# A hybrid decoder layer: the attention norm's scales are spread by DMA instead of by TensorE transposes

## What is computed

```python
h = rmsnorm(x, norm_g)
proj = h @ w_in                       # 1024 -> 8704, split in 12 pieces
y_a = (silu(layernorm(conv31(a_val * sigmoid(a_gate)))) * silu(a_z)) @ w_a_out
o = diff_attention(q, k, v, lam)      # 4 heads, causal: (softmax(q1 k1) - lam softmax(q2 k2)) v
o = rmsnorm(o, subln_g, 1e-5) * (1.0 - lam_init)   # over the 128 channels of a head
y_b = (o * silu(b_z)) @ w_b_out
y_c = (c_b * conv3(c_c * c_x) * silu(c_z)) @ w_c_out
merged = g0 * y_a + g1 * y_b + g2 * y_c            # sigmoid gates
out = rmsnorm(x + merged @ w_o, final_g)
```

## Time and profile before

| | us |
|---|---|
| median of 3 runs (2297.95 to 2299.34) | 2298.78 |
| the profiled execution | 2299.36 |
| its span, first to last instruction | 2297.6 |
| TensorE matmul busy, of the span | 2265.2 (99%) |
| VectorE busy | 1424.9 (62%) |
| ScalarE busy | 755.8 (33%) |
| GpSimd busy | 230.1 (10%) |
| mean granted TensorE clock | 0.999 |

### The profile page before, as it was taken

The page is one execution under the profiler, slowest core; times in us unless marked ns, Lnnn a source line. Parts: engine busy times, 40 slices in busy tenths (PEclk is TensorE's granted clock), DMA queues, the critical chain, the costliest instruction groups (busy, mean ns, idle before and its releaser), DMA issues.

```text
span 2297.6 us, 29108 instructions
## 1 busy us (share of the span) xinstructions
PE 2265.2 (99%) x10864; PEld 1836.2 (80%) x10864; DVE 1424.9 (62%) x2706; ACT 755.8 (33%) x1610; POOL 230.1 (10%) x186
## 2 busy tenths in 40 slices
PE   7999999999999999999999999999999999999998
PEld 6888888878888888888787787888877787778886
DVE  4767667774665665564566657665456656577752
ACT  4333332342333331022344344102135455441021
POOL 3545300100000000010000000001000000000010
PEclk9999999999999999999999999999999999999999
DMA  8877788788554545566644454456664444435555
GB/s 310 291 263 266 269 290 290 281 324 313 187 179 175 181 168 183 188 253 248 254 175 172 168 183 147 165 200 239 247 256 157 166 157 156 154 129 179 188 192 201
DMA packets 90604, 490.77 MB, mean 214 GB/s; under 512 B 9312, under 2 KB 9568, under 8 KB 45408
## 3 DMA queue, kind: packets, MB, share of 16 engines
q1 hardware_dynamic: 90464, 488.90, 59.6%
HBM read 375.61 MB, written 113.25 MB: 213 GB/s over the span
## 4 chain that ended last, share of the span: by engine, by line
PE 94%; DVE 3%; DMA 1%; issue 1%; ACT 0%; SPq 0%; DVEq 0%; ACTq 0%
PE PJ L733 73%; PE SC L792 6%; PE SC L824 5%; PE TB L833 3%; PE OB L857 1%; PE OB L858 1%; PE OB L792 1%; PE PJ L792 1%; PE OB L860 1%; PE OB L859 1%; DMA Wp<-split_weights 1%; PE TB L868 0%; DMA PX<-x_t 0%; DMA UC<-x 0%; PE TB L876 0%
## 5 line engine op out<-in xcount | busy, mean ns | idle before, releaser
L733 PE MATMUL PJ<-hT,Wp 128*128 128x512 f32 x6480 | 1577.4, 395 | 1.1 <-DMA Wp<-split_weights 0.6
L733 PEld LDWEIGHTS PJ<-hT,Wp 128*128 128x128 f32 x6480 | 1187.7, 188 | 254.0 <-issue 17.7
L1493 DVE SCALAR_TENSOR_TENSOR ACCS<-UA,col,ACCS 128x512 f32<-128x512 f32 x464 | 348.8, 793 | 0.4
L1030 ACT ACTIVATE PX<-SC,negm 128x512 f32<-128x512 f32 (+3 forms) x320 | 195.9, 623 | 153.3 <-DVE negm L1329 153.1
L1374 DVE TENSOR_TENSOR ZA<-TB,ZA 128x512 fp32r<-128x512 f32 (+1 forms) x144 | 95.0, 660 | 172.7 <-ACT ZA L1050 171.8
L1329 DVE TENSOR_REDUCE negm<-SC 128x2 f32<-128x1024 f32 (+3 forms) x160 | 168.9, 1061 | 43.0 <-PE SC L824 40.7
L1050 ACT ACTIVATE ZA<-TB 128x512 fp32r<-128x512 f32 (+1 forms) x144 | 82.5, 573 | 308.1 <-PE TB L833 308.1
L1089 ACT ACTIVATE TG<-PJ,col 128x512 f32<-128x512 f32 x64 | 44.1, 688 | 341.2 <-PE PJ L733 341.2
L1367 DVE SCALAR_TENSOR_TENSOR PX<-PX,sc 128x512 f32<-128x512 f32 (+3 forms) x160 | 105.4, 680 | 52.7 <-ACT PX L1041 52.1
L792 PE MATMUL SC<-Wp,KM 128*128 128x512 f32 x384 | 121.4, 389 | 0.0
L1041 ACT ACTIVATE PX<-PX,sc 128x512 f32<-128x512 f32 (+3 forms) x160 | 98.6, 655 | 64.6 <-DVE sc L1356 44.3
(11 more groups left out here) (191 smaller groups left out, 2044.6 us busy)
## 6 DMA issues: line engine op xcount, KB each, us to landing
Wp<-split_weights SPq DMA_DIRECT2D x264, 1024.0 KB, 4.8
split_weights<-Wp SPq DMA_DIRECT2D x88, 1024.0 KB, 4.9
Wraw<-w_stream SPq DMA_DIRECT2D x88, 512.0 KB, 5.9
KM<-keys SPq DMA_DIRECT2D x24, 512.0 KB, 5.7
VM<-values SPq DMA_DIRECT2D x24, 512.0 KB, 6.0
PX<-x SPq DMA_DIRECT2D x16, 512.0 KB, 7.0
out<-PX SPq DMA_DIRECT2D x16, 512.0 KB, 10.8
keys<-KM SPq DMA_DIRECT2D x12, 512.0 KB, 6.0
```

The costliest lines, as they stand in the source:

```text
L733: mm = pe.matmul(pj(c, r)[:, :], wt, rhs[:, 1 if q == 1 else 0, k, :], start=(n == 0), stop=(n == 3 * ktiles - 1))
L1030: a = act.activation(probs(c, h, t, j, m)[:, 0:w], SC[k][:, m, 0:w], ACT.Exp, bias=negm[:, t % 2, j, m:m + 1], accum_out=lsum[:, t % 2, j, ...
L1493: a = dve.scalar_tensor_tensor(out=acc, in0=src, scalar=col[:, n:n + 1], in1=acc, op0=ALU.mult, op1=ALU.add)
```

## The change

In chunks 1 to 3 the scales of all pairs but the last one, (3, 1), no longer pass TensorE. SyncE stores the 128 by 2 scales of the pair into a DRAM array of 2 by 128 (`store_scales`, a store of single elements) at lag `STORE_LAG`, and at lag `BACK_LAG` loads that row of 256 into all 128 partitions (`load_scales`) into `OV`, the first quarter of `Wraw[:, 1, :]`. VectorE multiplies from there, at lag 32 instead of 18 to 16, and the split follows at lags 33 and 34. The last pair of these chunks, "direct" in the code, is spread on TensorE as before, but earlier: lag 15 instead of 18, 17, 17. Chunk 0 keeps its lags and its transposes.

```diff
-SPREAD_LAG = (19, 18, 17, 17)
-ZB_LAG = (19, 18, 17, 16)
-ZBHI_LAG = (20, 18, 18, 17)
-ZBLO_LAG = (21, 19, 19, 18)
+STORE_LAG = (0, 14, 14, 13)
+BACK_LAG = (0, 24, 24, 24)
+ZB_LAG = (0, 32, 32, 32)
+ZBHI_LAG = (0, 33, 33, 33)
+ZBLO_LAG = (0, 34, 34, 34)
+
+DIRECT_SPREAD = (19, 15, 15, 15)
+DIRECT_ZB = (19, 16, 16, 16)
+DIRECT_HI = (20, 17, 17, 17)
+DIRECT_LO = (21, 18, 18, 18)
...
+def direct(c, h, q):
+
+    return c == 0 or (h, q) == (H - 1, 1)
...
-            for h, q in pairs_at(c, p - SPREAD_LAG[c]):
+            for h, q in direct_at(c, p, DIRECT_SPREAD):
                 order["s", c, h, q] = len(order)
...
+        OV = Wraw[:, 1, 0:2 * P]
...
+            def store_scales(c, h, q):
+
+                sp.wait_ge(on_ready, pair_at(c, h, q) + 1)
+                sp.dma_start(rs[stores_before(c, h, q), :, :].rearrange("i p -> p i"), ost[:, 5, :],
+                              allow_slow_non_contiguous=True).then_inc(scale_stored, 16)
+
+            def load_scales(c, h, q):
+                n = stores_before(c, h, q)
+                sp.wait_ge(scale_stored, 16 * (n + 1))
+                sp.dma_start(OV, rs[n:n + 1, :, :].rearrange("o i p -> o (i p)").to_broadcast([P, 2 * P])
+                              ).then_inc(scale_loaded, 16)
...
+                    for u in far_at(c, p, STORE_LAG):
+                        store_scales(c, *u)
+                    for u in far_at(c, p, BACK_LAG):
+                        load_scales(c, *u)
...
-                    for u in pairs_at(c, p - SPREAD_LAG[c]):
+                    for u in direct_at(c, p, DIRECT_SPREAD):
                         spread_o(c, *u)
...
+                if c > 0:
+                    wait(dve, scale_stored, 16 * stores_before(c, h, q))
                 dve.tensor_tensor(ost[:, 5, :], ost[:, 4, :], ost[:, 3, :], ALU.mult).then_inc(on_ready, 1)
 
             def zb_pair(c, h, q):
                 n, (OT, _, OG, ZF) = pair_at(c, h, q), pair_rooms(c)
-                dve.wait_ge(o_spread, n + 1)
                 wait(dve, zb_lo, n)
-                dve.scalar_tensor_tensor(out=ZF, in0=TB[:, 0:2 * P], scalar=col[:, COL_SG:COL_SG + 1], in1=OT,
-                                         op0=ALU.mult, op1=ALU.mult).then_inc(tb_free, 1)
+                if direct(c, h, q):
+                    dve.wait_ge(o_spread, spreads_before(c, h, q) + 1)
+                    dve.scalar_tensor_tensor(out=ZF, in0=TB[:, 0:2 * P], scalar=col[:, COL_SG:COL_SG + 1], in1=OT,
+                                             op0=ALU.mult, op1=ALU.mult).then_inc(tb_free, 1)
+                    dve.wait_ge(tb_free, TURN["s", c, h, q] + 1)
+                else:
+                    dve.wait_ge(scale_loaded, 16 * (stores_before(c, h, q) + 1))
+                    step(dve.scalar_tensor_tensor(out=ZF, in0=OV, scalar=col[:, COL_SG:COL_SG + 1], in1=OT,
+                                                  op0=ALU.mult, op1=ALU.mult))
                 dve.wait_ge(gate_copied, n + 1)
-                dve.wait_ge(tb_free, TURN["s", c, h, q] + 1)
                 dve.tensor_tensor(ZF, ZF, OG, ALU.mult).then_inc(zf_ready, 1)
```

More of the change, by code:

```diff
@@ L304, with direct_at, far_at, spreads_before @@
 SPARE = 14
+def direct(c, h, q):
+    return c == 0 or (h, q) == (H - 1, 1)
+def direct_at(c, p, lag):
+    return [u for u in pairs_at(c, p - lag[c]) if direct(c, *u)]
+def far_at(c, p, lag):
+    return [u for u in pairs_at(c, p - lag[c]) if not direct(c, *u)]
+def spreads_before(c, h, q):
+    return 2 * h + q if c == 0 else 2 * H + c - 1
+def stores_before(c, h, q):
+    return (2 * H - 1) * (c - 1) + 2 * h + q
+STORES = (2 * H - 1) * (NCHUNK - 1)
 def room_table(c):
@@ L385, with build @@
 TURN = turn_table()
-LAST_O = [max(TURN["s", c, h, q] for h in range(H) for q in range(2)) for c in range(NCHUNK)]
-def build(nc, x, x_t, w_stream, cols, final_g, lam_v, out, kd, vd, ws):
+LAST_O = [TURN["s", c, H - 1, 1] for c in range(NCHUNK)]
+def build(nc, x, x_t, w_stream, cols, final_g, lam_v, out, kd, vd, ws, rs):
     with ExitStack() as ctx:
@@ L493, in build @@
             sem("osum_done"), sem("ovar_ready"), sem("opow_done"), sem("on_ready"), sem("o_spread"), sem("zf_ready"))
-        o_copied, gate_copied = sem("o_copied"), sem("gate_copied")
+        o_copied, gate_copied, scale_stored = sem("o_copied"), sem("gate_copied"), sem("scale_stored")
+        scale_loaded = sem("scale_loaded")
         zb_hi, zb_lo = sem("zb_hi"), sem("zb_lo")
@@ L529, in pair_rooms @@
             if c > 0:
-                return [Wraw[:, 0, 2 * P * k:2 * P * (k + 1)] for k in range(4)]
+                return [Wraw[:, 0, k * 2 * P:(k + 1) * 2 * P] for k in range(4)]
             return [room(SPARE + k // 2)[:, k % 2 * 2 * P:(k % 2 + 1) * 2 * P] for k in range(4)]
+        OV = Wraw[:, 1, 0:2 * P]
         O2 = OB[:, :].rearrange("p (a n) -> p a n", a=2)
@@ L715, in _ @@
             sp.wait_ge(k_stored, 16 * H * (NCHUNK - 1))
+            sp.wait_ge(scale_stored, 16 * STORES)
             sp.wait_ge(v_stored, 16 * H * (NCHUNK - 1))
@@ L1157, in _ @@
                         o_square(c, *u)
-                    for u in pairs_at(c, p - ZBHI_LAG[c]):
+                    for u in far_at(c, p, ZBHI_LAG) + direct_at(c, p, DIRECT_HI):
                         zb_hi_pair(c, *u)
@@ L1251, in _ @@
                         o_power(c, *u)
-                    for u in pairs_at(c, p - ZBLO_LAG[c]):
+                    for u in far_at(c, p, ZBLO_LAG) + direct_at(c, p, DIRECT_LO):
                         zb_lo_pair(c, *u)
@@ L1676, in _ @@
                         o_scale(c, *u)
-                    for u in pairs_at(c, p - ZB_LAG[c]):
+                    for u in far_at(c, p, ZB_LAG) + direct_at(c, p, DIRECT_ZB):
                         zb_pair(c, *u)
@@ L1787 @@
     ws = nc.dram_tensor("split_weights", (W_CHUNK, P, 2, D), F32, kind="Internal").ap()
-    build(nc, *args, kd, vd, ws)
+    rs = nc.dram_tensor("output_scales", (STORES, 2, P), F32, kind="Internal").ap()
+    build(nc, *args, kd, vd, ws, rs)
     r = run_bass_kernel_spmd(nc, [{k: np.ascontiguousarray(a) for k, a in arrays.items()}], core_ids=[0])
```

## The result

The changed kernel takes 2286.79 us, median of five executions (2285.86 to 2286.82), against 2298.78 of the kernel before (2297.80 to 2299.43). The ratio is 0.9947, 95% interval 0.9933 to 0.9960. The gain is 12.0 us where 10.7 was forecast, and the time lies 0.01 us under the low end of the range. What was to leave TensorE left it, as forecast; the size and the range's low end did not come out, nor what the DMAs do on the way. The profiled execution took 2286.79 us, span 2285.0.

What follows compares the result with a forecast made beforehand. The prediction took TensorE, busy 99% of the span, as the bound. Savings of 4.6 (transposes), 2.2 (chunk 2's waits) and 3.9 (chunk 3's), all else 0, made 10.7 us: forecast 2288.1 us, range 2286.8 to 2290.5, chance 0.76.

Steps and rivals of the forecast that it cites:

- the range's low end: The forecast's own range began at 2286.8 us, allowing for small waits that shift, up to 2 us either way.
- Transposes, 21 x 0.22 = 4.6 us: In chunks 1 to 3, 21 pairs of transposes leave TensorE, each costing 0.22 us between starts: 4.6 us saved.
- Chunk 2's waits, 3 x 0.72 = 2.2 us: In chunk 2, heads 0 to 2, TensorE's 0.72 us wait for bank TB goes with the transposes: 2.2 us saved.
- Nothing takes this wait's place: In chunk 2, TB's next user comes three steps later, so no new wait replaces the 0.72 us one.
- Chunk 3's waits, 3 x 1.30 = 3.9 us: In chunk 3, heads 0 to 2, TensorE's 1.30 us wait for VectorE, late through the product's place, goes: 3.9 us saved.
- Moved product, last pairs: VectorE's 0.9 us product at lag 32 fits idle time; each chunk's last pair, spread earlier, neither waits nor gains: cost 0.
- The DMAs: cost 0: 21 stores and 21 loads on SyncE's queue make nothing wait, as weight loads have 6.2 us to spare.
- landings of L623 stay near 4.8: In the profile after, weight loads would still land about 4.8 us after issue.
- The sum of the late end: A store holding the rings 3.9 us plus a scale 1.8 us late makes 5.7, below the weights' spare of 6.2.
- signs of being wrong: TensorE waiting for weight loads, VectorE idle before its product for the scales' load, or chunk 3's gap staying.
- The rival in which element packets clog the queue: Slow store packets hold the rings 8.0 us, TensorE waits 1.8 us 21 times: 2326 us, chance 0.04.
- None of the rivals: Only transposes go (0.12), the moved product delays TensorE (0.06), packets clog the queue (0.04), transposes cost full duration (0.02).

Runs made afterwards that it cites:

- r1: The kernel before, unchanged, run and profiled a second time: 2298.64 us, ratio 0.9999.
- e2: The kernel before, transposes kept and no DMA added; only the lags of pairs (h, 1), heads 0 to 2, moved in chunks 2 and 3: 2299.47 us, ratio 1.0003.
- the repeat: Both kernels run again on one chip: the kernel before (r1), 2298.64 us, and the changed kernel (r2), 2286.62 us.
- e9: The changed kernel with five needless VectorE multiplications where the product used to stand in chunk 3: 2291.73 us, ratio 0.9970.
- e4: The changed kernel with three needless VectorE multiplications where the product used to stand in chunk 3: 2287.92 us, ratio 0.9951.
- r2: The changed kernel, unaltered, run and profiled a second time: 2286.62 us, ratio 0.9947.
- e5: The changed kernel with each of the 21 stores issued twice, the copy to another DRAM region: 2287.24 us, ratio 0.9954.
- e6: The changed kernel with scales stored as 128 rows of 8 bytes instead of 256 single elements: 2286.89 us, ratio 0.9952.
- e10: The kernel before plus 21 stores and no loads, the store's form differing in chunks 1, 2 and 3: 2298.88 us, ratio 1.0002.
- e7: The changed kernel with the single-element stores issued from ScalarE's queue, loads staying on SyncE: 2287.00 us, ratio 0.9953.
- e11: The changed kernel with each of the 21 stores issued four times, the copies to other DRAM regions: 2292.78 us, ratio 0.9972.

## Why the prediction missed its range

**Transposes, 21 x 0.22 = 4.6 us: mis-sized.** The seven pairs of chunk 1, where nothing else changes, cost 1.69 us, so 5.1 in all. The 0.22 was read at one pair and is right for a pair's own place (0.22 to 0.23); the 0.04 a head behind pair (h, 1) could not be seen there. What makes it isn't shown.

**Chunk 2's waits, 3 x 0.72 = 2.2 us: right.** 3 x 0.74 = 2.2 (2.1 against r1). e2 adds that a lag alone would have moved the wait, not removed it. "Nothing takes this wait's place" held for the change, not for any change that removes the wait.

**Chunk 3's waits, 3 x 1.30 = 3.9 us: right, a little small.** 1.47, 1.42 and 1.33, so 4.2, against the first profile; 4.0 against the repeat's. Its cause is shown from both sides: e2 took away part of the lateness and 0.65 to 0.77 us a head of the wait; e9 put it back and the wait returned.

**Moved product, last pairs: cost 0, right against the first profile.** Heads 5 to 7 are unchanged and head 4 differs by a pair's 0.22. Against the repeat, head 4 of chunk 3 is 0.31 longer instead, with the wait of 0.36 us shown above, so up to 0.5 us may be a cost that was put at nothing.

**The DMAs: cost 0 right, by a working that was wrong.** The store was to hold the rings at most 3.9 us, as 16 packets a ring at the queue's mean of 0.24 us. It lands at 8.8, and "landings of L623 stay near 4.8" holds for the median alone: behind a store they became up to 13.3. The upper bound was no bound, since it took packets to cost by number and mean. The sum of the late end, 5.7 us against 6.2 to spare, would have failed too, had it been made with the measured 8.8. The result held because the loads behind the stores had 7.9 to 14 us to spare and not 6.2: 0.83 us was left in one place, and 0.09 in e4. That it came out at 0 was partly luck. Two of the prediction's signs of being wrong, a wait for L623's loads and idle time before L1464, are absent from the first profile and show up once each, at 0.3 and 0.2 us, in r2 and e4. The rival in which element packets clog the queue had the right mechanism, even the size (8.0 us), and the wrong spare. The stores begin to cost with the second one (0.89 and 0.28 us in e5) and cost 6.0 with four, part of that by their issue.

**The sum and the range.** By parts it should have been 5.1 + 2.2 + 4.2 = 11.5, or 10.7 with r1 for the kernel before (5.1 + 2.1 + 4.0, less the 0.5 of head 4 in chunk 3); the forecast would have been 2287.3 to 2288.1. Measured: 12.0, and 12.0 to 12.3 in the repeat. What is left, 0.5 to 1.3 us, belongs to no step of the change that a head shows. The steps of single executions differ by more than that: 1.16 us at the start of chunk 2, and up to 1.9 in head 0 of chunk 0. Where the rest comes from stays open. The weight waits at the chunks' starts don't give it, as they are no rarer in the profiles with the change, but each profile is one draw.

**The step that failed** is the range's low end. The text named waits that shift by "up to 2 us either way", which from 2288.1 reaches to 2286.1, and then put the end at 2286.8, which is only 1.3 away. The time, 2286.79, is 0.01 under it. Beside it stand two terms of the sum that were too small, the transposes (4.6, measured 5.1) and the waits of chunk 3 (3.9, measured 4.0 to 4.2), and the 0.5 to 1.3 us that are in no term and stay open. None of the rivals was needed. That the miss is by 0.01 and not by nothing is chance: the repeat's median is 2286.62, that of e6 2286.89.

## What to carry to other kernels

Read the cost of a short TensorE instruction as a difference between starts, over many repeats, and at more than one place, since what surrounds it can add a few hundredths of a microsecond each time. Give the range at least the spread that you name yourself. When a bank that is shared makes an engine wait, moving its use by a step may only hand the wait to the next user; ask what stands ahead of the reader on its own engine. And judge a small store to DRAM by how long it holds the DMA engines for the loads behind it, not by its bytes or packets; here rows of more bytes, or pieces spread apart, held them less than elements side by side. Look at what those loads had to spare in more than one execution.

## What the runs showed of the hardware

- A store of 256 elements of 4 bytes, side by side in DRAM, lands in 8.8 us, and 128 of them in 8.7; 256 placed 512 bytes apart in 3.4; 128 rows of 8 bytes in 4.5 side by side and 1.4 apart (the change, e10, e6).
- Such a store delays the weight loads behind it from 4.8 to 11 us in chunk 1 and 13.3 in chunk 3 (the change), from ScalarE's queue as from SyncE's (e7: 11.6 in chunk 1). With the elements 512 bytes apart no load among the stores took over 5.7 (e10, chunk 1).
- Two or four such stores in a row to different places hardly take longer than one: median landings of 9.4 and 9.6 against 8.8 (e5, e11). But three more in a row took SyncE 4.45 us to issue, and the next load was issued 2.4 us later than with one (e11).
- After a wait of 2.94 us TensorE was granted a clock of 0.54 for the 3.2 us that followed, and the step cost 4.6 us (e11).
